# Inner features of the experts' down matrices reordered from k·128+p to 4p+k, with the gate and up products reading their moving columns at a step of four

## The reference, cut to what matters

```
hid = jax.nn.silu(jnp.einsum("nd,edf->nef", x, w_gate)) * jnp.einsum("nd,edf->nef", x, w_up)
y = jnp.einsum("nef,efd->nd", hid * gates[:, :, None].astype(hid.dtype), w_down)
```

## Time and profile before

| | us |
|---|---|
| median of 3 runs | 795.42 |
| lowest and highest run | 791.24, 796.65 |
| the profiled execution's own time | 793.16 |
| its span in the trace | 791.4 |
| TensorE busy, VectorE busy, ScalarE busy | 734.0, 237.2, 157.5 |
| data moved by DMA | 287.40 MB, mean 363 GB/s |

### The profile page before, as it was taken

The page is one execution under the profiler, slowest core; times in us unless marked ns, Lnnn a source line. Parts: engine busy times, 40 slices in busy tenths (PEclk is TensorE's granted clock), DMA queues, the critical chain, the costliest instruction groups (busy, mean ns, idle before and its releaser), DMA issues.

```text
span 791.4 us, 9516 instructions
## 1 busy us (share of the span) xinstructions
PE 734.0 (93%) x3745; PEld 345.0 (44%) x3745; DVE 237.2 (30%) x551; ACT 157.5 (20%) x408; POOL 73.1 (9%) x126
## 2 busy tenths in 40 slices
PE   4699899897999999998799999998999999998896
PEld 1345444455444443443234554454544434442432
DVE  0003544455310010100436228484501001000255
ACT  0201321325011110120103132343211101110201
POOL 0000000000200001102200110000200002101020
PEclk9899899997999999999999999999899999999998
DMA  8999999915499999999999999963299999999993
GB/s 324 397 322 410 410 409 419 417 77 213 186 420 416 417 422 415 421 416 416 419 399 379 409 410 418 397 239 144 98 420 416 422 418 416 422 416 419 415 409 116
DMA packets 67906, 287.40 MB, mean 363 GB/s; under 512 B 6636, under 2 KB 12268, under 8 KB 51988
## 3 DMA queue, kind: packets, MB, share of 16 engines
q1 hardware_dynamic: 63828, 275.54, 86.6%
q10 hardware_dynamic: 2880, 7.03, 2.2%
q0 software_dynamic: 1152, 4.19, 1.3%
HBM read 278.93 MB, written 7.82 MB: 362 GB/s over the span
## 4 chain that ended last, share of the span: by engine, by line
PE 51%; SPq 31%; DMA 9%; DVE 5%; ACT 2%; issue 2%; POOL 0%; DVEq 0%; ACTq 0%
PE bank L1171 14%; SPq L638 12%; PE bank L1207 7%; PE bank L987 7%; SPq L633 6%; DMA ring<-in_exp_w_up 6%; PE bank L838 5%; SPq L634 4%; PE bank L1138 4%; DMA ring<-in_w_mod 3%; PE bank L725 3%; SPq L598 3%; SPq L602 2%; PE bank L966 1%; PE bank L943 1%
## 5 line engine op out<-in xcount | busy, mean ns | idle before, releaser
L1171 PE MATMUL bank<-ring,arena 128*64 128x512 f32 x1024 | 226.2, 597 | 7.8 <-DMA ring<-in_exp_w_up 7.8
L1171 PEld LDWEIGHTS bank<-ring,arena 128*64 128x64 f32 x1024 | 73.5, 138 | 156.5 <-issue 151.5
L1207 PE MATMUL bank<-ring,arena 128*64 128x512 f32 x512 | 113.8, 595 | 6.8 <-DMA ring<-in_exp_w_down 5.7
L1787 DVE TENSOR_TENSOR arena<-bank,arena 128x256 f32<-128x256 f32 x32 | 13.6, 425 | 218.8 <-ACT arena L1993 218.5
L1207 PEld LDWEIGHTS bank<-ring,arena 128*64 128x64 f32 x512 | 36.3, 137 | 73.9 <-issue 66.0
L1138 PE MATMUL bank<-arena 128*128 128x128 f32 x512 | 63.5, 279 | 0.0
L1138 PEld LDWEIGHTS bank<-arena 128*128 128x128 f32 x512 | 61.1, 196 | 1.2 <-issue 0.7
L725 PE MATMUL bank<-ring,cwin 128*32 128x512 f32 x384 | 50.4, 665 | 11.0 <-DMA ring<-in_w_mod 10.4
L1884 ACT ACTIVATE arena<-bank 128x512 f32<-128x512 f32 (+5 forms) x65 | 34.8, 559 | 116.2 <-PE bank L838 32.6
L1993 ACT ACTIVATE arena<-bank 128x256 f32<-128x256 f32 x32 | 12.3, 383 | 219.2 <-PE bank L1171 219.2
L1803 DVE COPY arena<-bank 128x512 f32<-128x512 f32 x14 | 9.7, 691 | 121.9 <-PE bank L1207 121.9
(11 more groups left out here) (200 smaller groups left out, 652.7 us busy)
## 6 DMA issues: line engine op xcount, KB each, us to landing
ring<-in_exp_w_gate SPq DMA_DIRECT2D x62, 1024.0 KB, 20.6
ring<-in_exp_w_up SPq DMA_DIRECT2D x62, 1024.0 KB, 20.3
ring<-in_exp_w_down SPq DMA_DIRECT2D x60, 1024.0 KB, 22.5
ring<-in_w_mod SPq DMA_DIRECT2D x24, 2048.0 KB, 21.5
expert_rows<-arena ACTq DMA_DIRECT2D x12, 512.0 KB, 7.8
ring<-in_w_out_ab SPq DMA_DIRECT2D x2, 2048.0 KB, 23.6
ring<-in_exp_w_down SPq DMA_DIRECT2D x8, 512.0 KB, 15.0
ring<-in_w_in_c SPq DMA_DIRECT2D x2, 2048.0 KB, 18.0
```

Of the source, the lines that this page charges most:

```text
L1171: mm = nc.tensor.matmul(pb(key)[SLOTS * hf:SLOTS * (hf + 1), :], xeT[b][:, k * P + SLOTS * a:k * P + SLOTS * (a + 1)], w[:, :, k % 4, hf * ...
L1207: mm = nc.tensor.matmul(pb(key)[SLOTS * a:SLOTS * (a + 1), :], hp[:, c:c + SLOTS], w[:, a, kf % 2, hf * HALF:(hf + 1) * HALF], start=(kf = ...
```

## The change

A down matrix is now read with inner feature 4p+k on partition p, so that two neighbouring k are one 8 KB piece of memory. So that the hidden product comes out in the same order, the gate and up matmuls no longer take 256 neighbouring columns of each matrix: half hf takes the features 4m+r for r = 2hf and 2hf+1 and m = 0 to 127. The block's view has the order (w, r, m) with m at a step of four elements (16 bytes). Instruction counts, tiles, semaphores, sizes and the order of the loads stay; the last two loads at line 629 keep pieces of 2 KB.

```diff
-        w_down = i_["exp_w_down"].rearrange("l e (k p) c -> (l e) p k c", p=P)
+        w_down = i_["exp_w_down"].rearrange("l e (p k) c -> (l e) p k c", p=P)
...
-        w_down_k = i_["exp_w_down"].rearrange("l e (k p) c -> (l e) k p c", p=P)
+        w_down_k = i_["exp_w_down"].rearrange("l e (p k) c -> (l e) k p c", p=P)
...
-                    w = block_ap(n + k // 4).rearrange("p (w k f) -> p w k f", w=2, k=4)
+                    w = block_ap(n + k // 4).rearrange("p (w k m r) -> p w k r m", w=2, k=4, r=4)
                     for hf in range(2):
                         mm = nc.tensor.matmul(pb(key)[SLOTS * hf:SLOTS * (hf + 1), :],
                                               xeT[b][:, k * P + SLOTS * a:k * P + SLOTS * (a + 1)],
-                                              w[:, :, k % 4, hf * 256:(hf + 1) * 256],
+                                              w[:, :, k % 4, 2 * hf:2 * hf + 2, :],
                                               start=(k == 0), stop=(k == KD - 1))
...
-                                            w.rearrange("p (w f) -> p w f", w=2)[:, :, hf * 256:(hf + 1) * 256],
+                                            w.rearrange("p (w m r) -> p w r m", w=2, r=4)[:, :, 2 * hf:2 * hf + 2, :],
```

## The result

| | before | after |
|---|---|---|
| median, us (4 runs each) | 795.33 | 1018.8 |
| lowest and highest | 791.24, 796.65 | 1018.09, 1019.99 |
| span of the profiled execution | 791.4 | 1017.3 |
| ratio, 95% interval | | 1.2822 (1.2774 to 1.2871) |

The change makes the kernel 28% slower. The page of the changed kernel says where: its span, the busy tenths and the DMA rate in 40 slices, the queues, and the lines that the chain passes through.

The account below looks back on a forecast made before the run. Loads bound the expert stages, with TensorE nearly the bound. Line 1171's 111.1 us more per layer, less 14.5 us idle, gave + 207.7 on 795.4, so 1003 us; the 8 KB pieces' 2.5 us vanish. Range 787 to 1030.

Parts of the forecast that it names:

- The bound: Expert stages: loads bound them, TensorE nearly does, idle only 7.7 and 6.8 us, 14.5 us in all.
- the case of 927 to 1030 us: Gate and up products: a step costs TensorE what ScalarE's copies show, + 143 to + 244 ns an instruction; chance 0.60.
- The rows: Down loads in 8 KB pieces: 421 instead of 412.5 GB/s, 2.5 us saved, only while loads bound the stage.
- The step: Line 1171, moving columns at a step of four: + 217 ns an instruction, 111.1 us more TensorE work a layer.
- The second ground: Moving operand of line 1171: an element comes in the next turn or misses it, hence a value near the upper end.
- Free reading: Moving-operand reader: the step costs TensorE nothing and only the 8 KB pieces count, 793 us (788 to 797); chance 0.30.
- The count that spoke against it: Moving-operand reads: two tiles at step four touch 1024 16-byte pieces in 434 ns, four tiles on neighbours 512 in 444.
- the third rival: Gate and up products: both tiles share one reader, + 651 ns an instruction, near 1447 us; chance 0.04 for above 1030.
- The small cost: Line 1171: between 15 and 143 ns more an instruction, 842 us at + 60 ns; chance 0.06 for 800 to 927.

Follow-up runs that it names:

- the version that reads pairs: Against the changed kernel, each half reads two neighbouring features of every four and VectorE reorders the hidden product when writing; 793.5 us, ratio 0.999.
- the rows alone: Against the kernel before, only the down matrices come in 8 KB rows, moving columns stay neighbours; 792.48 us, ratio 0.9967.
- the step alone: Against the kernel before, only the gate and up moving columns are read at a step of four, down matrices keep 4 KB pieces; 1019.8 us.
- the half-by-half rows: Against the kernel before, 8 KB down pieces within each half of the features, TensorE reads neighbours, VectorE reads at a step of two; 791.49 us, ratio 0.9963.

## Why the prediction was right

**The bound.** The prediction held TensorE to be within 14.5 us of being the bound, with no more to absorb a loss. So it came: 13.5 of the 14.5 us went, and the rest of the longer line 1171 lengthened the stages one for one. A pair takes 40.0 us, with 39 forecast; DMA fell to 306 and 256 GB/s in the stages, with 320 forecast for both. The stated range, 787 to 1030, spans a free step and a dear one and would have held either; the forecast to test is the case of 927 to 1030 us, held at 0.60, and its likeliest value.

**The rows.** Taken at 2.5 us (0 to 5); alone they gave 2.6 us (1.1 to 4.1 by the interval). The wait that was to shorten did so by 1.3 and 1.1 us in the version that reads pairs. With the rows alone another wait, for a down matrix, came to end last, which the prediction didn't see. It was forecast that they are worth nothing once the step makes TensorE the bound; the step alone took 1019.8 us in its one run, against 1018.8 with the rows, which is no difference.

**The step.** This is the term that was too small. The prediction took one turn of 0.85 ns more for an element, 217 ns for an instruction. The chain shows 28.80 instead of 13.73 us for 64, so 450 instead of 215 ns (the prediction's base of 217 is that of a stage's first 64), 235 ns more, 0.92 ns an element; it lay inside the two ends taken from ScalarE's copies (143 and 244 ns), near the upper. Line 1171's busy time grew by 119.8 and 118.1 us where 111.1 were forecast for each layer; these 15.7 us are nearly what the forecast of 1003 us lacks.

The direction and the bound were reasoned, the closeness of the size was partly luck. The ground for the value was an inference from a neighbour, ScalarE writing at a step of 128 elements where TensorE reads at a step of four; that the two costs are alike in size doesn't show that they have one cause, and no run here tests ScalarE. The second ground, that an element comes in the next turn or misses it, didn't hold: the measured costs are 10, 55, 216, 235, 244 and 267 ns, of which only that of the step of 32 is a whole turn. If a piece of 16 bytes takes 1.76 ns, that this is near two turns of 0.84 ns is a coincidence of the two numbers. And the prediction's words would also have priced a step of two, at which the cost is 10 ns.

**The rivals.** Free reading fell with line 1171 at 450 ns; its argument, that the reader has reserve because four streams draw twice the elements, was beside the point, since each stream has its own limit. The count that spoke against it, pieces of 16 bytes instead of elements, points at the right unit, but it summed over streams, and the limit isn't in that sum: four streams at a step of four touch twice as many pieces in the same time as two do (line 729 above). Blocking among the streams, the third rival, fell with the same run. The small cost exists, but for other patterns: 10 ns with two elements in each 16 bytes, 55 ns in the alternation by 512 bytes.

## What to carry to other kernels

Before a layout is changed to make a transfer better, ask what reads the data at which step: 2% on a third of the loads was paid here with a doubled time on the most frequent instruction. On TensorE's moving operand in float32, as measured here, a step of two elements is nearly free and a step of four doubles the instruction. If an order must change somewhere, split the index so that the transfer's piece and the wide reader's run both stay whole, and put the rearrangement in a small operation that has time, as the half-by-half rows did with VectorE's product.

## What the runs showed of the hardware beyond the forecast

- A stream of 512 float32 on TensorE's moving side took 430 ns for neighbours, about 450 ns with two elements from each 16 bytes, 540 ns when two places 512 bytes apart, each read through in order, were visited in turn, and 862 to 964 ns with one element from each 16 bytes.
- With one, two or four column tiles beside each other a stream at a step of four took about the same 900 ns: 900, 450 and 225 ns for an instruction.
- VectorE's product of 256 columns took 421 ns when it read both inputs at a step of two and wrote neighbours, and 612 ns when it wrote at a hop of 512 bytes.
- The down pieces of 8 KB brought the mixed load stream from 418 to 421 or 422 GB/s.
